# Gated hybrid block on one core: bias skew in eight parts, the first spatial mix two steps later, odd values a step later, and the low half of turned softmax blocks made by GpSimd

## What is computed

```python
h = rms_norm(x, pre_norm); proj = h @ w_in
q, k, v, gate_a, u_b, v_b, gate_b, mg_a, mg_b = split(proj)
o_a = sliding_window_attention(q, k, v, sinks, rel_bias)     # 16 heads of 64, window 128, T5 bias, sink
y_a = (o_a * silu(gate_a)) @ w_branch_a
o_b = gelu(u_b) * (tril(w_spatial) @ layer_norm(gelu(v_b)) + b_spatial)   # chunks of 128
y_b = (o_b * silu(gate_b)) @ w_branch_b
out = (sigmoid(mg_a) * y_a + sigmoid(mg_b) * y_b) @ w_out
return x + rms_norm(out, post_norm)
```

## Time and profile before

| | us |
|---|---|
| median of 3 runs | 910.57 (908.77 to 911.44) |
| the profiled execution, its own time | 908.92 |
| its span, first to last instruction | 907.2 |
| PE busy in the span | 894.8 (99%) |
| PE weight loads busy | 746.9 (82%) |
| DVE, ACT, POOL busy | 671.5, 500.9, 498.2 |
| granted TensorE clock, mean over the span | 0.998 of full |

### The profile page before, as it was taken

How to read it: one execution, slowest core, us unless ns; L and a number is a source line. 1 busy time by engine, 2 the same in 40 slices (tenths; PEclk the granted TensorE clock), 3 DMA queues, 4 the chain that set the end, 5 groups by cost and what they waited for, 6 DMA issues and landing times.

```text
span 907.2 us, 12749 instructions
## 1 busy us (share of the span) xinstructions
PE 894.8 (99%) x4268; PEld 746.9 (82%) x4268; DVE 671.5 (74%) x1167; ACT 500.9 (55%) x982; POOL 498.2 (55%) x395
## 2 busy tenths in 40 slices
PE   9999999999999999999999989999999999999997
PEld 7888788888888888888888868888888888888886
DVE  6766695576666666757576669688689878989968
ACT  6554254775767676666767664334443434534563
POOL 3564235777787777787869636445542252043236
PEclk9999999999999999999999999999999999999999
DMA  8788764433434346534343443533289550435004
GB/s 311 194 201 241 240 209 105 136 104 86 134 88 127 95 117 163 150 105 117 102 116 103 116 146 105 186 117 123 62 292 334 185 209 1 139 114 211 1 1 185
DMA packets 170512, 130.90 MB, mean 144 GB/s; under 512 B 58552, under 2 KB 139472, under 8 KB 170320
## 3 DMA queue, kind: packets, MB, share of 16 engines
q1 hardware_dynamic: 168208, 126.66, 45.7%
q10 hardware_dynamic: 2240, 3.43, 1.2%
HBM read 93.87 MB, written 39.35 MB: 147 GB/s over the span
## 4 chain that ended last, share of the span: by engine, by line
PE 84%; DVE 5%; ACT 4%; issue 3%; SPq 2%; DMA 1%; POOL 0%; DVEq 0%; POOLq 0%; ACTq 0%
PE acc L1019 42%; PE acc L1200 11%; PE ps_m L1200 7%; PE ps_t L1200 7%; PE acc L872 7%; PE ps_t L1036 2%; PE acc L962 2%; PE ps_m L1067 2%; SPq L506 1%; ACT prob L1570 1%; DVE neg_s L2137 1%; DVE pt_pack L2151 1%; ACT prob L1578 1%; DVE ps_t L2134 1%; PE ps_t L1046 1%
## 5 line engine op out<-in xcount | busy, mean ns | idle before, releaser
L1019 PE MATMUL acc<-mv,w_hi 128*128 128x512 f32 x1344 | 353.8, 392 | 0.0
L1019 PEld LDWEIGHTS acc<-mv,w_hi 128*128 128x128 f32 x1344 | 244.8, 188 | 44.9
L1019 PE MATMUL acc<-mv,w_lo 128*128 128x512 f32 x672 | 182.0, 393 | 0.0
L1813 POOL TENSOR_TENSOR w_lo<-sums,w_hi 128x1024 fp32r<-128x1024 f32 x48 | 118.0, 2460 | 73.1 <-ACT w_hi L1366 48.9
L1019 PEld LDWEIGHTS acc<-mv,w_lo 128*128 128x128 f32 x672 | 126.7, 189 | 28.6
L1813 POOL TENSOR_TENSOR w_lo<-raw,w_hi 128x1024 fp32r<-128x1024 f32 (+1 forms) x48 | 95.2, 1984 | 40.1 <-ACT w_hi L1359 32.6
L1570 ACT ACTIVATE prob<-neg_s,neg_max 128x129 f32<-128x129 f32 x128 | 50.5, 396 | 89.7 <-DVE neg_max L2137 89.6
L1200 PE MATMUL acc<-right,left 128*128 128x512 f32 x432 | 98.7, 389 | 0.0
L1200 PEld LDWEIGHTS acc<-right,left 128*128 128x128 f32 x432 | 81.0, 188 | 17.2 <-DVE left L2203 0.4
L2151 DVE TENSOR_TENSOR pt_pack<-turned_in,pt_pack 128x256 fp32r<-128x256 f32 x32 | 43.6, 1362 | 42.5 <-ACT pt_pack L1588 42.5
L1857 POOL TENSOR_SCALAR_AFFINE_SELECT pt_prev<-pt_pack 128x512 fp32r<-128x512 f32 x64 | 40.8, 638 | 58.6 <-DVE pt_pack L2127 39.8
(11 more groups left out here) (286 smaller groups left out, 1688.0 us busy)
## 6 DMA issues: line engine op xcount, KB each, us to landing
raw<-in_w_in SPq DMA_DIRECT2D x56, 512.0 KB, 4.5
ht_d<-sums SPq DMA_DIRECT2D x8, 512.0 KB, 4.9
mix_d<-mix_b SPq DMA_DIRECT2D x8, 512.0 KB, 4.0
prob_d<-prob SPq DMA_DIRECT2D x32, 128.0 KB, 2.2
turned_in<-prob_d SPq DMA_DIRECT2D x128, 32.0 KB, 2.2
ga_d<-gate SPq DMA_DIRECT2D x16, 256.0 KB, 4.1
tb<-tb_d SPq DMA_DIRECT2D x4, 1024.0 KB, 5.1
ub<-mix_d SPq DMA_DIRECT2D x7, 512.0 KB, 3.4
```

The lines of the kernel that those rows point to most:

```text
L1019: ins = nc.tensor.matmul(bank, (w_lo if y == 2 else w_hi)[:, left + k * P:left + (k + 1) * P], right[:, (OPW if y == 1 else 0) + k * HALF: ...
L1813: nc.gpsimd.tensor_tensor(w_lo[:, c], src, w_hi[:, c].bitcast(f32), ALU.subtract).then_inc(wlo_ok, 1)
```

## The change

Four edits are made together.

- The bias is skewed by two heads. `skew(p)` is one copy for head pair p. ACT's queue issues the first where it issued the whole before; SP issues the one for p + 1 at k = 7 of head pair p, and `load_bias` waits for it.
- For pair 16 alone, `u_mix` moves from step 3 to step 5, and `u_mul` of the first half from step 4 to step 5.
- PE's values of odd blocks move from lag 5 to lag 6.
- The low half of the even (turned) blocks is no longer made by DVE at lag 5, but by POOL at lag 6, in front of its mask. SP's `prob_back` now waits for POOL's instruction and not for DVE's before it overwrites `turned_in`, and `ptl_ok` counts the odd blocks alone.

```diff
+        def skew(p):
+
+            return (skew_d[2 * p:2 * p + 2, :, :],
+                    bass.AP(bias_d, 2 * p * BIAS_ROW, [[BIAS_ROW, 2], [0, P], [1, BIAS_ROW]]))
...
             def load_bias(p):
-                if p == 0:
-                    sp.wait_ge(bias_out, 32)
-                else:
+                sp.wait_ge(bias_out, 32 + 16 * p)
+                if p:
                     sp.wait_ge(scores_used, 8 * p)
...
                 sp.wait_ge(prob_out, 16 * (j + 1))
                 if j:
-                    sp.wait_ge(ptl_ok, 2 * j)
+                    sp.wait_ge(pool_own, POOL_FRONT + j)
...
+                if k == 7 and p + 1 < HEAD_PAIRS:
+                    sp.dma_start(*skew(p + 1)).then_inc(bias_out, 16)
...
-                for blk in odd_at(k, 5) + even_at(k, 7):
+                for blk in odd_at(k, 6) + even_at(k, 7):
                     values(p, blk)
...
-                    act.dma_start(skew_d[:, :, :], bass.AP(bias_d, 0, [[BIAS_ROW, N_HEADS], [0, P], [1, BIAS_ROW]])).then_inc(bias_out, 16)
+                    act.dma_start(*skew(0)).then_inc(bias_out, 16)
...
+                for blk in even_at(k, 6):
+                    pool.wait_ge(turn_hi, 4 * p + blk // 2 + 1)
+                    pack = pt_pack[0]
+                    nc.gpsimd.tensor_tensor(pack[:, 256:512], turned_in[:, :], pack[:, 0:256].bitcast(f32),
+                                            ALU.subtract).then_inc(pool_own, 1)
                 for blk in even_at(k, 6) + odd_at(k, 3):
-                    pool.wait_ge(ptl_ok, place(p, blk))
+                    if blk % 2:
+                        pool.wait_ge(ptl_ok, 4 * p + blk // 2 + 1)
+                    else:
+                        pool.wait_ge(pool_own, POOL_FRONT + 4 * p + blk // 2 + 1)
...
-                for blk in even_at(k, 5):
-                    dve.wait_ge(turn_hi, 4 * p + blk // 2 + 1)
-                    pack = pt_pack[0]
-                    nc.vector.tensor_tensor(pack[:, 256:512], turned_in[:, :], pack[:, 0:256].bitcast(f32),
-                                            ALU.subtract).then_inc(ptl_ok, 1)
...
-                    if kind(n) == "U" and n < PAIRS - 1:
+                    if FIRST_U < n < PAIRS - 1:
                         u_mix(n)
...
-                    if kind(n) == "U":
+                    if n > FIRST_U:
                         u_mul(n, 0)
...
+                if s == 5 and n == FIRST_U:
+                    u_mix(n)
+                    u_mul(n, 0)
```

More of the change, by code:

```diff
@@ L1043, in transpose_p @@
                 if s > 1:
-                    pe.wait_ge(ptl_ok, place(p, blk) - 2)
+                    pe.wait_ge(ptl_ok, 4 * p + blk // 2)
                 for h in range(2):
@@ L1174, in square_unit @@
                     pe.wait_ge(oadd_ok, 4 * HEAD_PAIRS)
-                    pe.wait_ge(ptl_ok, 8 * HEAD_PAIRS)
+                    pe.wait_ge(ptl_ok, 4 * HEAD_PAIRS)
+                    pe.wait_ge(pt_ok, 8 * HEAD_PAIRS)
                 if x == 2 and not st and i == 0:
@@ L1827, in rsqrt_out @@
                     nc.gpsimd.tensor_scalar(msq_o[:, :], ssq_o[:, 0:NT], EPS, 1.0, ALU.add, ALU.mult).then_inc(pool_own, 1)
-                    pool.wait_ge(pool_own, POOL_FRONT + 1)
+                    pool.wait_ge(pool_own, POOL_FRONT + 4 * HEAD_PAIRS + 1)
                 pool.wait_ge(osq_ok, NT + j + 1)
                 nc.gpsimd.tensor_tensor(msq_o[:, r:r + 1], msq_o[:, r:r + 1], ssq_o[:, NT + r:NT + r + 1], ALU.add).then_inc(pool_own, 1)
-                pool.wait_ge(pool_own, POOL_FRONT + j + 2)
+                pool.wait_ge(pool_own, POOL_FRONT + 4 * HEAD_PAIRS + j + 2)
                 nc.gpsimd.tensor_tensor(rstd_o[:, r:r + 1], msq_o[:, r:r + 1], neg_half[:, :], ALU.pow).then_inc(ors_ok, 1)
```

## The result

The change made the kernel slower, by 0.6%. The changed kernel takes 915.73 us in the median of six runs (912.2 to 917.36), the kernel before 910.02 in six beside them (908.52 to 911.44): ratio 1.0058, 95% interval 1.0037 to 1.008. The profiled execution took 917.36 with a span of 915.6, and its parts are compared with the 908.92 and 907.2 of before. It is the slowest of its six, and that of before is 1.1 us under its median: the two profiles lie 8.4 us apart, the medians 5.7. So the main prices read from profiles are given by the timed runs as well.

A forecast was written before the change was run, and what follows sets the result against it. PE was taken as the bound, busy 894.8 of 907.2 us, so only its waits could be won. 3.38 + 1.4 + 0.5 + 1.08 = 6.4, plus 0.5 for brackets, 6.9: 903.7 us in the median, range 901 to 908.5.

The forecast's parts named there:

- the price of the seven copies on SP: SP's queue, k = 7: 384 KB copies land in 4 us; the even block's way out has over 4 us; price 0.
- Rival D: SP's queue: copies hold the even block's way out, ACT stands about 5 us seven times; 938 us, chance 0.03.
- first mix later: Pair 16: PE's 3.38 us wait before the transposes and the clock's 1.4 us go; gain 4.8 us.
- low half on POOL: Before pair 16's scores: 0.5 of PE's 0.79 us wait goes; POOL's instruction takes 0.74 us, hidden price 0.
- odd values later: PE's values of odd blocks, one step on: 0.45 us of work moves; price 0, gain 0.
- bias in the front: Front: the load of x issues 6.9 us earlier, PE's 1.08 us wait behind DVE goes; gain 1.1 us.
- the sum: Whole kernel: waits and clock give 6.4 us, brackets 0.5, together 6.9 us.

The follow-up runs named there:

- the spread copy: The changed kernel with the bias copy's 128 repeated rows outermost and the two heads inside, over all DMA engines: 901.25 us at k = 7, 900.84 at k = 12.
- the repaired kernel: The changed kernel with the bias copy's 128 repeated rows as outermost dimension, over all DMA engines, at k = 7: 901.25 us.
- the kernel with two narrow copies in ACT's queue: The changed kernel with the two-engine copy for p + 2 issued at k = 12, ACT's queue making the first two in the front: 934.84 us.
- three repaired forms: The changed kernel with the copy over all engines at k = 7 (901.25 us), at k = 12 (900.84), or in two two-engine halves (901.37).

## Why the prediction was wrong

The step that failed is the price of the seven copies on SP. The prediction put it as a landing between 15.8 / 8 = 2 us and 15.8, took 4, and wrote price 0 behind "leaves over 4 us in the way out". It scaled the old copy by its bytes and took the bias tile as neighbour, and so assumed that the new copy spreads over the engines as those do. It does not: 8.2 us on two engines, the way out landing 11.6 us after its issue, 16.2 us of the pairs (542.8 against 526.6 with the spread copy) in the profiled executions, about 14.3 by the ratios of the timed runs. The waits of the page account for 10.8 of it, the two dips of the clock for some 3; seven brackets that each understate by 0.16 us add 1.1; the rest, about 1, was not located. Spread, the copy lands 5.4 to 6.8 us after its issue, where 4 was taken, and the price is the 0 that was forecast: what failed is the assumption on its width.

Rival D named the mechanism, at 0.03: the copy holds the way out, and ACT stands for it. It decided from a landing of some 8 us on and at 15.8 us expected 5 us at each of seven places. The copy's last packet ended 11.6 us after its issue (282.62 to 294.17), and each place cost 2.3 (16.2 / 7). What D got wrong was the reason for which it was put aside, the bytes. Its sum is 938.7 and not 938.

Term by term, with pairs and front from the profiled executions:

| term | forecast gain | measured |
|---|---|---|
| first mix later | 3.4 + 1.4 clock + 0.16 bracket = 4.9 | 4.6 (528.6 against 533.2) |
| low half on POOL | 0.5 + 0.16 bracket | 1.0 up to pair 16, 2.0 together with odd values |
| odd values later | 0 | 1.0 up to pair 16; as a whole not told from before |
| bias in the front | 1.08 + 0.16 bracket | first product 0.9 to 1.6 earlier in the six kernels with the split bias at k = 4 or 7 |
| seven copies in SP's list | 0 | -16.2 (-14.3 by the timed runs) |

*The first mix.* Right in mechanism and size: no idle time in front of the transposes, the granted clock 1.00 from 531 to 538 in the repaired kernel, and `u_mix` with no idle time ahead of it:

```profile
530.42 1.28 DVE L2182 SCALAR_TENSOR_TENSOR ub<-ub,g_col 128x1024 f32<-128x1024 f32 x1
```

*The low half.* The duration was right (0.74 us), no mask was late by it, and the wait for the maximum fell from 0.8 to 0.4. That POOL's instruction is longer than DVE's at its best (0.42) cost PE nothing here. The gain was undersized: the two edits gave 2.0. Only 0.4 of it stands as a wait of PE; the rest comes in pieces of up to 0.4 us over the pairs, none of which the profile lists as a wait, and about 1.0 of it comes from the odd values, which I had at nothing. Why matmuls stand closer with the values a step later was not settled.

*The front.* The load behaved as forecast only with the copy spread: 5.7 us to issue with an eighth of the bytes. In the changed kernel, where that eighth went over two engines, it took 10.09. That the slow load is the whole cause of PE's wait is not shown: at 10.09 PE's wait behind DVE was gone as well, and with the whole bias again it was 12.20 with a wait of 0.2. The worth is not one number either, because with the whole bias the pairs' first product starts at 137.6, 138.4, 138.5, 139.6 or 142.3 us in the five executions profiled, without it at 136.8 to 137.5 (leaving out the kernel with two narrow copies in ACT's queue). The latest of these, 142.3, had waits of 2.5 and 1.4 us in the front, and the clock at its lower level for 3.4 us behind them. In the timed runs the edit alone gave 2.0.

With the copy repaired, the change as a whole gives what the sum said and more, in part by luck, since low half and odd values were put too low and the mix a little too high: 7.5 us in the span (907.2 to 899.7) for 6.9, and 8.2 to 9.0 in the timed runs of three repaired forms. The fastest is the spread copy, 901.25 us at k = 7 and 900.84 at k = 12; these two ran at different times and can't be told apart.

## What to carry to other kernels

Price a transfer by its shape and not by its bytes: look at the outermost dimension of both sides, and when a copy is cut into pieces, see to it that each piece still has a dimension there that all DMA engines can share. A wait that names a compute engine should be followed back through the chain until a queue appears: here PE named POOL, POOL ACT, ACT a landing, and the queue an issue of 3.98 us. When several edits go in together and the sum fails, repair the suspected one before removing any; it told in one run that the rest together were a gain of the size forecast.

## What had not been expected of the hardware

- A transfer on two engines delays those behind it in its queue, though the DMA view shows a share of one to two tenths meanwhile: issue 3.98 us for 0.56, landing 11.6 for 2.9, and at k = 12 weights' loads of 512 KB that land after 10.2 us, with ACT standing 6.57. Half the rows (4.1 us at 48 GB/s) left the issue at 0.83 us.
- The same wait of 3.4 to 3.5 us costs differently by the clock. Before, the granted share was 0.55 for 3.1 us and then full; with the odd values alone it was 0.50 and 0.52 over 6.1 us. In the kernel with only the spread bias, PE's wait ended at 533.73 and full clock came only in the third of these rows:

```profile
534.00:537.00 3.00, 3.00 (x9) 2.42 (x9) 2.49 (x6) 2.94 (x6) 0.64 (x1) 0.50 0.15 35
537.00:540.00 3.00, 3.00 (x12) 2.44 (x12) 1.51 (x2) 2.75 (x4) 2.61 (x3) 0.65 0.45 87
540.00:543.00 3.00, 3.00 (x17) 2.57 (x16) 3.00 (x3) 1.78 (x4) 3.00 (x2) 1.00 0.66 208
```

So a profile with such a wait is uncertain by 1 us or more. Removing the wait does not remove all scatter: the kernel with only the mix moved has it no more, and its six runs still lie between 903.3 and 907.6 us. Where those 4 us come from no trace here shows, since only its 904.37 was profiled.
